# A gated multi-branch mixer layer on one core: the output projection by seven block products for eight

## The reference

```
proj = x @ w_in                      # 1024 x 9480, split among the branches
y_a  = (swish(LN(conv31(glu(a)))) * silu(gate_A)) @ p_a
y_b  = (b * conv3(c * h) * silu(gate_B)) @ p_b
y_c  = (forgetting attention, 8 heads of 64, * silu(gate_C)) @ p_c
y_m  = (attention into 256 memory tokens, 4 heads, * silu(gate_M)) @ p_m
merged = sum_i sigmoid(g_i) * y_i    # per channel, i = A, B, C, M
out  = merged @ w_out                # 1024 x 1024 by 1024 x 1024
x    = LayerNorm(alpha * x + out) * ln_g + ln_b
```

## Time and profile before

| | |
|---|---|
| time, median of 3 runs (lowest, highest) | 1217.01 us (1216.97, 1217.59) |
| the profiled execution: its own time | 1218.22 us |
| the profiled execution: span from first to last instruction | 1216.4 us |
| PE busy | 1197.8 us, 98% |
| DVE, ACT, POOL busy | 790.7, 545.2, 708.0 us |
| mean granted TensorE clock | 0.998 of full speed |

### The profile page before, as it was taken

The page is one execution under the profiler, slowest core; times in us unless marked ns, Lnnn a source line. Parts: engine busy times, 40 slices in busy tenths (PEclk is TensorE's granted clock), DMA queues, the critical chain, the costliest instruction groups (busy, mean ns, idle before and its releaser), DMA issues.

```text
span 1216.4 us, 15836 instructions
## 1 busy us (share of the span) xinstructions
PE 1197.8 (98%) x5736; PEld 999.9 (82%) x5736; DVE 790.7 (65%) x1284; ACT 545.2 (45%) x998; POOL 708.0 (58%) x555
## 2 busy tenths in 40 slices
PE   7999999999999999999999999999999999999997
PEld 6888888888888888888888888888888888878886
DVE  4623765677576674428897666676667686776755
ACT  5433433344443444547475556655655444315000
POOL 5677887887777777878446444455542225648000
PEclk9999999999999999999999999999999999999999
DMA  9022131232323323233512011111102533376131
GB/s 279 1 70 66 39 104 35 70 136 93 118 105 104 128 93 126 104 105 121 191 54 64 25 53 53 36 53 53 29 7 96 191 130 105 100 268 231 72 127 69
DMA packets 91277, 118.61 MB, mean 98 GB/s; under 512 B 6072, under 2 KB 72632, under 8 KB 91200
## 3 DMA queue, kind: packets, MB, share of 16 engines
q1 hardware_dynamic: 91200, 117.60, 29.5%
HBM read 92.39 MB, written 25.20 MB: 97 GB/s over the span
## 4 chain that ended last, share of the span: by engine, by line
PE 88%; DVE 7%; issue 2%; ACT 2%; DMA 1%; POOL 1%; DVEq 0%; SPq 0%; ACTq 0%
PE pj L758 11%; PE pj L760 11%; PE pj L759 11%; PE pj L829 5%; PE pj L830 5%; PE pj L831 5%; PE pj L1098 4%; PE pt L760 3%; PE pt L758 3%; PE pt L759 3%; PE po L943 3%; PE pj L846 2%; PE pj L847 2%; PE pj L848 2%; PE po L1098 2%; PE pt L1098 2%
## 5 line engine op out<-in xcount | busy, mean ns | idle before, releaser
L1607 POOL TENSOR_TENSOR ring_lo<-w_pair,ring_hi 128x512 fp32r<-128x512 f32 x168 | 232.6, 1386 | 111.4 <-ACT ring_hi L1154 111.2
L1660 POOL TENSOR_TENSOR w_lo<-w_raw,w_hi 128x128 fp32r<-128x128 f32 (+1 forms) x104 | 111.5, 1092 | 138.1 <-ACT w_hi L1244 136.0
L1154 ACT ACTIVATE ring_hi<-w_pair 128x512 fp32r<-128x512 f32 x168 | 105.1, 628 | 160.6 <-PE pj L760 108.6
L1829 DVE SCALAR_TENSOR_TENSOR po<-glu,cwa,po 128x512 f32<-128x512 f32 x232 | 159.4, 746 | 20.6 <-ACT po L1205 20.6
L758 PE MATMUL pj<-t_hi,ring_hi 128*128 128x512 f32 x392 | 152.8, 390 | 0.3 <-DVE slot L1793 0.3
L760 PE MATMUL pj<-t_hi,ring_lo 128*128 128x512 f32 x392 | 152.5, 389 | 0.0
L759 PE MATMUL pj<-t_lo,ring_hi 128*128 128x512 f32 x392 | 152.5, 389 | 0.0
L829 PE MATMUL pj<-xT_hi,w_hi 128*128 128x512 f32 x320 | 126.2, 394 | 0.0
L830 PE MATMUL pj<-xT_lo,w_hi 128*128 128x512 f32 x320 | 125.3, 392 | 0.0
L831 PE MATMUL pj<-xT_hi,w_lo 128*128 128x512 f32 x320 | 125.1, 391 | 0.0
L1708 POOL TENSOR_SCALAR probs<-probs,rinv 128x128 f32<-128x128 f32 (+3 forms) x32 | 57.9, 1811 | 107.9 <-DVE rinv L2148 107.9
(11 more groups left out here) (364 smaller groups left out, 2992.1 us busy)
## 6 DMA issues: line engine op xcount, KB each, us to landing
w_pair<-in_w_in SPq DMA_DIRECT2D x28, 1024.0 KB, 5.2
gate_scratch<-slot SPq DMA_DIRECT2D x16, 1024.0 KB, 4.0
gate<-gate_scratch SPq DMA_DIRECT2D x32, 512.0 KB, 3.7
w_raw<-in_w_in SPq DMA_DIRECT2D x20, 512.0 KB, 3.9
z_scratch<-slot SPq DMA_DIRECT2D x8, 512.0 KB, 2.6
bias<-cum_scratch SPq DMA_DIRECT2D x8, 512.0 KB, 3.7
wout_raw<-in_w_out SPq DMA_DIRECT2D x8, 512.0 KB, 5.4
x_tok<-in_x SPq DMA_DIRECT2D x8, 512.0 KB, 4.3
```

What stands on the lines that cost most here:

```text
L1154: nc.scalar.activation(ring_hi[:, j % RING, :, :], w_src(u, p), ACT.Copy).then_inc(s_rhi, 1)
L1607: nc.gpsimd.tensor_tensor(ring_lo[:, j % RING, :, :], w_src(u, p), ring_hi[:, j % RING, :, :], ALU.subtract).then_inc(s_rlo, 1)
L1660: nc.gpsimd.tensor_tensor(w_lo[:, j % 2, k, :], w_raw[:, j % 2, k, :], w_hi[:, j % 2, k, :], ALU.subtract).then_inc(s_wlo, 1)
L1829: nc.vector.scalar_tensor_tensor(out=acc if n < PAD_A else src, in0=src, scalar=cwa[:, ct, n:n + 1], in1=acc, op0=ALU.mult, op1=ALU.add).t ...
```

## The change

**Output projection.** The 1024 x 1024 by 1024 x 1024 product is done by 4 units of 256 tokens. Each unit has seven products in the order 1, 5, 6, 2, 7, 3, 4, each of 4 blocks k by three matmuls (12 matmuls of 512 columns), where four output tiles took 96 matmuls. Operands are `merged` (128 tokens by 512 channels) or a sum of such (`merged_sum`), in a ring of five (ACT `out_ring_hi`, POOL `out_lo`), and seven 512 x 512 blocks of `w_out` or of sums of its blocks (`ob_raw`, `ob_hi`, `ob_lo`, 0 to 6 in the order of first use). Products 1, 5 and 6 are copied by ACT (`out_copy`), added to `x_tok` by DVE (`with_copy`), and the banks go on accumulating products 7, 3 and 4.

**w_out's sums.** DVE makes 16 sums of 128 x 512 (`block_sum`) in pairs 3 and 5 of the input projection, from rows that SP loads; SP stores them to DRAM and loads the seven blocks later (1 MB each), among the p tiles M5 to C7.

**Splitting the blocks.** ACT makes `ob_hi` (`out_block_hi`), then copies the block to four PSUM banks (`out_block_copy`), and DVE subtracts from those copies (`out_block_lo`): blocks 0 to 3 among the last p tiles, blocks 4, 5 and 6 within the first output unit, by banks 2 and 3 in turn.

**Last p tiles.** C6 and C7 run half by half (C6 h0, C7 h0, C6 h1, C7 h1) and DVE adds them; DVE also makes the first three sums of unit 0. The adds of M1, M3, M5, M7 go from DVE to POOL.

**Start.** 12 matmuls on a constant tile (set by DVE) stand ahead of the first product; the first weight rows are issued from ACT's queue, and DVE casts the first block of x.

**Smaller.** The gate of the first A tile is loaded earlier; in the tail `L2377`'s pass stands before the reciprocal, and in the last unit the normalisation of tile 6 stands before the last result.

```diff
+    O_RING = 5
+    OUT_B = {1: 0, 5: 1, 6: 2, 2: 3, 7: 4, 3: 5, 4: 6}
+    LAST_C = S_END - 2
...
+                if s == S_OF[BR_C, 2]:
+                    load_out_block(1)
+                if s == S_OF[BR_C, 4]:
+                    load_out_block(2)
+                if s == S_OF[BR_C, 6]:
+                    sp.wait_ge(s_addm, ADDM_NO[S_OF[BR_M, 4]])
+                    sp.wait_ge(s_add, ADD_NO[S_OF[BR_M, 5]])
+                    load_out_block(3)
+                if s == S_OF[BR_C, 7]:
+                    load_out_block(4)
+                if s == S_END:
+                    load_out_block(5)
+                if s == S_END + 1:
+                    sp.wait_ge(s_pj, 2 * S_OF[BR_M, DT - 1] + 2)
+                    load_out_block(6)
+            sp.wait_ge(s_pj, 2 * S_END)
...
+        def block_bank(n, k):
+            return bank(4 + k if n < 4 else 2 + k % 2)
...
+        def merged_sum(eng, ops, u, n):
+            a11, a12, a21, a22, s1 = (out_src(u, p) for p in (1, 2, 7, 4, 5))
+            if n == 1:
+                eng.wait_ge(s_addc, 2 + 2 * (u // 2))
+                if u:
+                    eng.wait_ge(s_orl, OSLOT[u - 1, 5] + 1)
+                    eng.wait_ge(s_osum, O_SUM_NO[u - 1, 2])
+                dst, in0, in1, op = s1, a21, a22, ALU.add
+            elif n == 3:
+                eng.wait_ge(s_osum, O_SUM_NO[u, 1])
+                dst, in0, in1, op = a21, a11, a21, ALU.subtract
+            elif n == 2:
+                eng.wait_ge(s_osum, O_SUM_NO[u, 3])
+                eng.wait_ge(s_orl, OSLOT[u, 1] + 1)
+                dst, in0, in1, op = a11, s1, a11, ALU.subtract
+            else:
+                eng.wait_ge(s_osum, O_SUM_NO[u, 2])
+                eng.wait_ge(s_orl, OSLOT[u, 2] + 1)
+                dst, in0, in1, op = a12, a12, a11, ALU.subtract
+            ops.tensor_tensor(dst, in0, in1, op).then_inc(s_osum, 1)
...
+            for _ in range(12):
+                nc.tensor.matmul(bank(7), warm[:, 0:P], warm[:, :], start=True, stop=True)
...
+            for h in range(2):
+                for s in range(LAST_C, S_END):
+                    pe.wait_ge(s_pjfree, 2 * s + h - 3)
+                    p_steps(s, h, 0, CT, 2 * ((s + 1) % 2) + h)
...
+            def out_product(j):
+                u, p = OSEQ[j]
+                if p == 1:
+                    if u == 2:
+                        pe.wait_ge(s_obl, KH * 7)
+                    elif u == 3:
+                        pe.wait_ge(s_yk, 1)
+                elif p == 5:
+                    if u == 1:
+                        pe.wait_ge(s_pjfree, 2 * S_END)
+                    elif u >= 2:
+                        pe.wait_ge(s_yk, 4 * (u - 1))
+                elif p == 6:
+                    pe.wait_ge(s_ocp, 3 * u + 1)
+                elif p == 2:
+                    if u == 3:
+                        pe.wait_ge(s_yk, 3)
+                elif p == 7:
+                    pe.wait_ge(s_ocp, 3 * u + 3)
+                elif p == 3:
+                    pe.wait_ge(s_ocp, 3 * u + 2)
+                else:
+                    pe.wait_ge(s_yk, 4 * u + 2)
+                pe.wait_ge(s_orl, j + 1)
+                if u == 0:
+                    pe.wait_ge(s_obl, max(16, KH * (OUT_B[p] + 1)))
+                dst = out_bank(u, p)
+                for k in range(KH):
+                    w_h, w_l = o_ring_hi[j % O_RING][:, k, :], o_ring_lo[j % O_RING][:, k, :]
+                    hi, lo = ob_hi[OUT_B[p]][:, k, :], ob_lo[OUT_B[p]][:, k, :]
+                    nc.tensor.matmul(dst, w_h, hi, start=k == 0 and p in (1, 2, 5), stop=False, skip_group_check=True)
+                    nc.tensor.matmul(dst, w_h, lo, start=False, stop=False, skip_group_check=True)
+                    mm = nc.tensor.matmul(dst, w_l, hi, start=False, stop=k == KH - 1, skip_group_check=True)
+                mm.then_inc(s_out_pj, 1)
...
+                act.dma_start(w_pair[u][:, 0, :], first_w_rows(u, 0)).then_inc(s_x11[0], 16)
...
+            def out_block_hi(n):
+                act.wait_ge(s_wo[n], 16)
+                if n == OUT_B[3]:
+                    act.wait_ge(s_pj, 2 * S_OF[BR_M, DT - 1] + 2)
+                elif n == OUT_B[4]:
+                    act.wait_ge(s_pj, 2 * S_END)
+                nc.scalar.activation(ob_hi[n][:, :, :], ob_raw[n][:, :, :], ACT.Copy, scale=0.5).then_inc(s_obh, 1)
...
+            def out_block_copy(n):
+                for k in range(KH):
+                    if n == 0:
+                        act.wait_ge(s_zpre, CT + MP)
+                        act.wait_ge(s_pjfree, 2 * S_OF[BR_B, DT - 1] + 2)
+                    elif n < 4:
+                        act.wait_ge(s_obl, KH * (n - 1) + k + 1)
+                    elif n == 4 and k < 2:
+                        act.wait_ge(s_pjfree, 2 * S_END)
+                    else:
+                        act.wait_ge(s_obl, KH * n + k - 1)
+                    nc.scalar.activation(block_bank(n, k), ob_raw[n][:, k, :], ACT.Copy, scale=0.5).then_inc(s_obc, 1)
...
+                if S_END - 5 <= s:
+                    out_block_hi(s - (S_END - 5))
+                if S_END - 5 <= s < S_END - 1:
+                    out_block_copy(s - (S_END - 5))
+            for j in range(O_RING):
+                out_ring_hi(j)
+                if j == 2:
+                    out_block_copy(4)
+            for u in range(OU):
+                for p in ORDER:
+                    if p in (1, 5, 6):
+                        out_copy(u, p)
+                    if u and p == 5:
+                        out_std(2 * u - 1)
+                    if OSLOT[u, p] + O_RING < NOQ:
+                        out_ring_hi(OSLOT[u, p] + O_RING)
+                    if u == 0 and p in (5, 6):
+                        out_block_hi(p)
+                        out_block_copy(p)
+                    if p == 4:
+                        out_std(2 * u)
+            out_std(NT - 1)
...
+            for u in range(OU):
+                for p in ORDER:
+                    if p == 1 and u:
+                        merged_sum(pool, nc.gpsimd, u, 1)
+                        merged_sum(pool, nc.gpsimd, u, 3)
+                    out_lo(OSLOT[u, p])
+                    if p == 1 and u:
+                        merged_sum(pool, nc.gpsimd, u, 2)
+                    if p == 2:
+                        merged_sum(pool, nc.gpsimd, u, 4)
...
+            def block_sum(k, n):
+                b11, b12, b21, b22 = (ob_rows[k % 2][:, q // 2, q % 2 * HALF:(q % 2 + 1) * HALF] for q in range(4))
+                if n == 0:
+                    dve.wait_ge(s_wor, 64 * (k // 2 + 1))
+                else:
+                    dve.wait_ge(s_ot, 4 * k + n)
+                dst, in0, in1 = ((b11, b12, b11), (b12, b22, b12), (b22, b22, b11), (b21, b21, b22))[n]
+                nc.vector.tensor_tensor(dst, in0, in1, ALU.subtract).then_inc(s_ot, 1)
...
+            nc.vector.memset(warm[:, :].bitcast(mybir.dt.uint32), 127 << 23).then_inc(s_warm, 1)
...
+            nc.vector.tensor_copy(xT_hi[:, 0, 0, :], r11[:, 0, :]).then_inc(s_xbh, 1)
...
+                    if u in (3, 5) and 2 <= i < 6:
+                        for n in range(2):
+                            block_sum(u - 3 + (i - 2) // 2, i % 2 * 2 + n)
...
-                if br == BR_M:
+                if br == BR_M and dt % 2 == 0:
...
+                if s >= LAST_C:
+                    dve.wait_ge(s_pjfree, half_no(s, h))
+                    dve.wait_ge(*added(S_OF[BR_M, dt]))
+                    nc.vector.tensor_tensor(merged[:, dt, hs(h)], merged[:, dt, hs(h)], gate, ALU.add).then_inc(s_addc, 1)
...
+            def out_block_lo(n):
+                dve.wait_ge(s_obh, n + 1)
+                for k in range(KH):
+                    dve.wait_ge(s_obc, KH * n + k + 1)
+                    nc.vector.tensor_tensor(ob_lo[n][:, k, :], block_bank(n, k), ob_hi[n][:, k, :],
+                                            ALU.subtract).then_inc(s_obl, 1)
...
+                if s >= S_OF[BR_C, 2]:
+                    out_block_lo(s - S_OF[BR_C, 2])
+            for h in range(2):
+                for s in range(LAST_C, S_END):
+                    p_half(s, h, 2 * ((s + 1) % 2) + h)
+                if h == 0:
+                    for n in (1, 3, 2):
+                        merged_sum(dve, nc.vector, 0, n)
+            for n in range(4, 7):
+                out_block_lo(n)
...
+            def with_copy(u, p):
+                q, h = {1: (0, 0), 5: (1, 1), 6: (0, 1)}[p]
+                dve.wait_ge(s_xtk[q], 16 * (u + 1))
+                dve.wait_ge(s_ocp, 3 * u + {1: 1, 5: 2, 6: 3}[p])
+                v = x_tok[:, q, hs(h)]
+                nc.vector.scalar_tensor_tensor(out=v, in0=v, scalar=ALPHA, in1=o_cp[p][:, :], op0=ALU.mult,
+                                               op1=ALU.add).then_inc(s_pre, 1)
...
+            for u in range(OU):
+                for p in (1, 5, 6):
+                    with_copy(u, p)
+                for p in (2, 7, 3):
```

(56 more changed lines are left out.)

291 lines of the change are left out of this document (156 added, 135 removed).

## The result

The changed kernel takes **1226.54 us** (median of 6 runs, 1226.36 to 1227.24) against 1217.48 us (6 runs) for the kernel before: ratio 1.0076, 95% interval [1.0064, 1.0088], slower by 9 us. 1219.0 was forecast, with 1223.0 as the upper end.

A forecast was written before the change was run, and what follows sets the result against it. PE was taken as the bound, busy 1197.8 of 1216.4 us. Terms -10.9 + 11.5 + 1.1 + 2.1 + 0.7 - 0.3 - 2.2 = +2.0 us on the median 1217.01 gave 1219.0 us, range 1211.8 to 1223.0.

The forecast's parts named there:

- 48 matmuls: Output projection: 336 matmuls for 384, 0.227 us each, -10.9 us, the only large gain.
- start: Kernel start: constant matmuls raise the clock before the real ones, -2.2 us (-3.0 to +0.4).
- pairs 5 and 6: Input projection: six w_out sums in pair 5 delay results that pair 6 needs, +2.1 us (0 to +4).
- M and C tiles: p tiles: POOL's four adds between weight splits, block 0's load ahead of M4's gate, +0.7 us (-0.5 to +2).
- first A tile's gate: Earlier load of the first A tile's gate removes small waits, -0.3 us.
- first output unit, waits up to product 4: PE waits 2.3, 2.6 and 6.6 us at products 6, 7 and 4: +11.5 us (+8.3 to +14).
- matmuls at the lower clock behind them: First output unit: the prediction's sum has no term for a lower clock behind the waits.
- tail: After the last matmul: normalisation of tile 6 stands before the last result, +1.1 us (0 to +2.1).
- C7's gate is still late: Slower rival, before the first output unit: gate lands 3 us later, +3.0, 1222.0 us; chance 0.10.
- The ports hardly meet: Faster rival, DVE against POOL: first unit costs 8.3, pair 5 0.7, total -2.6, 1214.4 us; chance 0.27.
- The clock rises no earlier: Slower rival, kernel start: +0.4 us for -2.2, 1221.6 us; chance 0.13.
- The low end: Whole kernel: 1211.8 us, with first unit 8.3, pair 5 0, M tiles -0.5, start -3.0.

The follow-up runs named there:

- run 2: Changed kernel with 14, 12 and 18 spare matmuls ahead of products 6, 7 and 4 of the first output unit: 1227.21 us.
- run 12: Changed kernel with w_out's sums placed earlier (1222.62 us), plus 14, 4 and 24 spare matmuls ahead of products 6, 7 and 4: 1221.11 us.
- Run 5: Changed kernel with w_out's 16 sums at other places in VectorE's queue, rows stored and reloaded one pair earlier: 1222.62 us.
- run 6: Changed kernel with the adds of M1, M3, M5 and M7 on VectorE again: 1228.76 us.
- run 11: Kernel with early sums, C5's add on VectorE and reordered queues (1214.49 us), with blocks 0 to 2 loaded one or two places later: 1215.75 us.
- run 1: Kernel before with the start edits alone (12 constant matmuls, first weight rows from ACT's queue, first cast on DVE): 1214.54 us, ratio 0.9978.
- run 14: Kernel with early sums, C5's add on VectorE and reordered queues (1214.49 us), with blocks 0 to 2 copied once more to DRAM: 1220.21 us.

## Why the prediction was wrong, by its own steps

| term | forecast | measured in the traces |
|---|---|---|
| 48 matmuls | -10.9 | -10.9 (stage 86.8 to 91.4 us, gaps 10.7, slow matmuls 4.6) |
| start | -2.2 | -2.45 (16.84 for 19.29) |
| pairs 5 and 6 | +2.1 | +3.7 (gaps 3.3, slow ones 0.35) |
| M and C tiles | +0.7 | +1.4 (M tiles 26.3 us for 25.1, C tiles 33.0 for 32.8) |
| first A tile's gate | -0.3 | -0.3 |
| first output unit, waits up to product 4 | +11.5 | +12.2 |
| matmuls at the lower clock behind them | nothing | +3.1 |
| tail | +1.1 | +1.2 |
| sum | +2.0 | +8.0 (spans: +8.2) |

**The step that failed** is the first output unit's: its sum of +11.5 took PE's waits as the whole price, with matmuls at 0.227 us behind them, and so put the lower clock behind the waits at nothing, where it measured +3.1. Of the 6.0 us between the forecast's +2.0 and the +8.0 measured that is half; pairs 5 and 6 are 1.6, and the first unit's waits and the M and C tiles 0.7 each. The chain itself came nearly as written. C7's gate was there at 1121.7, or 1119.3 on the clock of before, for 1118.9; product 6, 7 and 4 began at 1130.5, 1138.8 and 1150.2 on that clock for 1129.2, 1137.2 and 1149.3, a copy into PSUM took 0.58 to 0.60 us, and three `with_copy` took 4.05 where 2.1 + 2.6 was taken. Most of the lateness is the third sum (1.82 us beside POOL for 0.69). Product 4 should have begun at 1124.14 + 16.32 = 1140.46 and did at 1152.66: 12.2. But the clock fell. Product 7's ten slow matmuls (1.7 us) are hidden in the third wait, which DVE's queue ends; the fourteen from product 4 on (2.6 us) are not, and with single late starts this makes 15.3 - 12.2 = 3.1. I had used the clock's level for the start and not asked what waits of 2.6 to 4.1 us do to it in the middle. The Trainium skill (TensorE: Matmul & The Clock Gate, Part 1) says that the array is throttled by default, that activity releases it, and that a wait between bursts of matmuls can throttle it again. By that rule this was to be expected, and runs 2 and 12 agree: with matmuls in the waits the clock stays at 1.00, and 1.5 to 3.1 us come back. Why the clock fell behind the second wait and not behind the longer first one stays open.

**Pairs 5 and 6** were rightly placed and under-sized: 1.55 us a sum for 1.19, since nearly each one met GpSimd, and a sum of slots behind them too (1.66 us for 0.69). By the prediction's own way 1.55 a sum gives 9.3 - 3.3 - 1.7 = 4.3, near the 3.7 measured; its upper bound of +4 is short of what a full POOL op for each sum would give. Run 5 shows the cause.

**M and C tiles**: of the two causes I gave, GpSimd's adds were wrong (run 6) and the early load on SP's queue was right and under-sized: with blocks 0 and 1 later the M tiles are 2.5 us shorter (run 11's trace). The net is only +1.2 there, since the waits for gates, which I took to stay, fell from 2.1 to 1.2 us, as they do with the start edits alone (run 1, 0.9). That more bytes there cost more, run 14 shows.

**Of the rivals**, "C7's gate is still late" did not hold as priced: it was there 0.4 us later than forecast, not 3.0. "The ports hardly meet" was wrong: the 16 sums took 1.47 us in the mean and the 12 `with_copy` 1.41, for 0.69 alone. "The clock rises no earlier" was wrong in this trace: the first real matmuls came at 0.227. That the point of the rise varies between runs, as the prediction had it, the traces bear out: the first 48 products ended between 16.67 us (run 5) and 18.01 (run 1). None of the rivals held a lower clock in the middle. (The low end is 1211.7 by its own terms, not 1211.8.)
